# Hybrid decoder step on one core: three of the twelve expert pair loads of the middle rounds are issued by ScalarE instead of SyncE

## What is computed

```
g_logits = (xn @ w_rg) + b_rg;  grp = argmax(g_logits)          # 4 groups
top_v, top_i = top_k(e_logits[grp], 2)                          # 2 of the group's 8 experts
for g in range(4):
    h = silu(einsum('nd,edf->nef', xn, w_gate[g])) * einsum('nd,edf->nef', xn, w_up[g])
    out = out + einsum('nef,efd->nd', h * combine[:, g, :, None], w_down[g])
y = rmsnorm(x + out, g_final)
```

## Time and profile before

| | us |
|---|---|
| median of 3 runs | 1608.3 (1607.51 to 1609.42) |
| time of the profiled execution | 1609.79 |
| span of the profiled execution | 1608.1 |
| TensorE busy | 1423.5 (89%) |
| VectorE busy | 562.4 (35%) |
| ScalarE busy | 407.5 (25%) |

### The profile page before, as it was taken

One profiled execution on the slowest core, in us unless ns is written; L12 is line 12 of the kernel. 1 busy time (PEld: TensorE's weight loads), 2 busy tenths in 40 slices (PEclk: granted clock), 3 DMA queues, 4 the chain that ended last, 5 costly groups with the idle time before them and its releaser, 6 DMA issues.

```text
span 1608.1 us, 24033 instructions
## 1 busy us (share of the span) xinstructions
PE 1423.5 (89%) x9911; PEld 936.3 (58%) x9911; DVE 562.4 (35%) x923; ACT 407.5 (25%) x680; POOL 13.8 (1%) x30
## 2 busy tenths in 40 slices
PE   7999999999999999999977778878878778967967
PEld 7999999999999999963332232322322322412411
DVE  5647765554555555532212112111112111111114
ACT  6454344333333344401201101101102002002003
POOL 0000000000000010000000000000000000000000
PEclk9999999999999999999979989989889888989889
DMA  8777445545555659699999999999999999999997
GB/s 322 301 282 271 148 164 181 180 179 183 182 183 183 255 204 362 235 393 426 431 432 428 433 433 425 436 432 430 432 431 430 430 430 430 431 432 430 434 428 298
DMA packets 42513, 544.73 MB, mean 339 GB/s; under 512 B 5825, under 2 KB 5825, under 8 KB 11593
## 3 DMA queue, kind: packets, MB, share of 16 engines
q1 hardware_dynamic: 42322, 544.03, 82.8%
q10 hardware_dynamic: 144, 0.03, 0.0%
HBM read 540.30 MB, written 3.68 MB: 338 GB/s over the span
## 4 chain that ended last, share of the span: by engine, by line
PE 62%; DMA 34%; DVE 1%; ACT 1%; issue 1%; SPq 0%; DVEq 0%; ACTq 0%
DMA ring<-in_expert_chunks 29%; PE bank L1524 12%; PE bank L1525 12%; PE bank L1526 12%; PE bank L1931 6%; PE bank L1934 5%; DMA side<-in_expert_chunks 4%; PE bank L1811 3%; PE bank L1866 2%; DMA ring<-in_dense_units 1%; PE bank L1858 1%; PE bank L1803 1%; PE bank L1854 1%; PE bank L1847 1%; PE bank L1555 0%
## 5 line engine op out<-in xcount | busy, mean ns | idle before, releaser
L996 DVE TENSOR_TENSOR w_lo<-ring,w_hi 128x1024 fp32r<-128x1024 f32 x220 | 259.8, 1222 | 223.3 <-ACT w_hi L726 222.8
L1524 PE MATMUL bank<-xn_hi,w_hi 128*128 128x264 f32 x1120 | 319.0, 285 | 0.0
L1525 PE MATMUL bank<-xn_lo,w_hi 128*128 128x264 f32 x1120 | 317.3, 283 | 0.0
L1526 PE MATMUL bank<-xn_hi,w_lo 128*128 128x264 f32 x1120 | 317.1, 283 | 0.0
L726 ACT ACTIVATE w_hi<-ring 128x1024 fp32r<-128x1024 f32 x220 | 221.1, 1052 | 367.2 <-PE bank L1526 342.6
L1931 PE MATMUL bank<-side 128*32 128x512 f32 x1024 | 153.5, 741 | 84.4 <-DMA side<-in_expert_chunks 83.4
L1524 PEld LDWEIGHTS bank<-xn_hi,w_hi 128*128 128x128 f32 x1120 | 210.9, 188 | 1.2 <-issue 1.0
L1525 PEld LDWEIGHTS bank<-xn_lo,w_hi 128*128 128x128 f32 x1120 | 211.1, 188 | 0.1
L1526 PEld LDWEIGHTS bank<-xn_hi,w_lo 128*128 128x128 f32 x1120 | 210.0, 187 | 0.0
L1811 PEld LDWEIGHTS bank<-trunk,x_all 128*128 128x128 f32 (+1 forms) x672 | 98.8, 202 | 77.7 <-issue 59.4
L1931 PEld LDWEIGHTS bank<-side 128*32 128x32 f32 x1024 | 33.9, 129 | 178.9 <-DMA side<-in_expert_chunks 98.3
(11 more groups left out here) (309 smaller groups left out, 1640.7 us busy)
## 6 DMA issues: line engine op xcount, KB each, us to landing
ring<-in_expert_chunks SPq DMA_DIRECT2D x33, 4096.0 KB, 33.9
side<-in_expert_chunks SPq DMA_DIRECT2D x28, 4096.0 KB, 38.7
ring<-in_dense_units SPq DMA_DIRECT2D x109, 1024.0 KB, 4.8
trunk<-in_expert_chunks SPq DMA_DIRECT2D x13, 4096.0 KB, 42.9
ring<-in_expert_chunks SPq DMA_DIRECT2D x20, 2048.0 KB, 14.5
ring<-in_expert_chunks SPq DMA_DIRECT2D x18, 1024.0 KB, 18.3
side<-in_expert_chunks SPq DMA_DIRECT2D x8, 2048.0 KB, 10.7
trunk<-in_expert_chunks SPq DMA_DIRECT2D x7, 2048.0 KB, 17.0
```

What stands on the lines that cost most here:

```text
L996: V.tensor_tensor(w_lo[n % 2][:, js, :], raw[n % 2][:, js, :], w_hi[n % 2][:, js, :], ALU.subtract).then_inc(lo_done, 1)
L1524: mm(ps[:, 0:n], w_hi[b][:, j, :], x_hi[:, j, :], start=j == k0, stop=False)
L1525: mm(ps[:, 0:n], w_hi[b][:, j, :], x_lo[:, j, :], start=False, stop=False)
L1526: ins = mm(ps[:, 0:n], w_lo[b][:, j, :], x_hi[:, j, :], start=False, stop=j == k1 - 1)
```

## The change

Of the seven loads in the first loop of SyncE's middle rounds q8 is left out, and of the five in the second q2 and q3; they are issued by ScalarE on its own hardware DMA queue. q4, which stood behind q2 and q3 in SyncE's order and needed no wait there, now waits for chunk 19. ScalarE issues q8 of the round when chunk 7 is used, ahead of the Silu; q2 of the next round after its copy n = 2 (so after chunk 21), q3 after its copy n = 3 (after chunk 23). ScalarE's loop is split into a first round, a loop over the middle ones, and a last round; the first and the last issue no load. The bytes, the places and TensorE's program stay as they are.

```diff
+BY_ACT = (8, 2, 3)
...
                     for q in range(5, PAIRS):
-                        pair_after(q, FREED_BY[q], at, bass.ds(r, 1))
+                        if q not in BY_ACT:
+                            pair_after(q, FREED_BY[q], at, bass.ds(r, 1))
                     for q in range(5):
-                        pair_after(q, AHEAD[q], at, bass.ds(r + 1, 1))
+                        if q not in BY_ACT:
+                            pair_after(q, 19 if q == 4 else None, at, bass.ds(r + 1, 1))
...
+            def pair_by_act(q, round_of):
+
+                s = PAIR_SLOT[q]
+                act.sem_inc(second_in[q], 16)
+                act.dma_start(pair[s].rearrange("p (o n) -> p o n", o=1), pair_v[:, q, round_of, :]).then_inc(full[s], 16)
+
+            def act_round(it, this=None, next=None):
+
+                act.wait_ge(e_used, it * CPR + (CREDIT + 8))
+                if this is not None:
+                    pair_by_act(8, this)
+                nc.scalar.activation(hs, bank[0][:, :], ACT.Silu, scale=slot_rms).then_inc(silu_done, 1)
+                for n in range(4):
+                    act.wait_ge(e_used, it * CPR + (CREDIT + 18 + 2 * n))
+                    if n:
+                        act.wait_ge(sq_done, it * 9 + (3 * n + 1))
+                    nc.scalar.activation(y[:, n % 2, :], bank[2 + n][:, :], ACT.Copy).then_inc(y_ready, 1)
+                    if n >= 2 and next is not None:
+                        pair_by_act(n, next)
...
             with act.Fori(0, npass) as k:
...
+                act_round(k * ROUNDS)
+                with act.Fori(1, ROUNDS - 1) as r:
+                    act_round(k * ROUNDS + r, bass.ds(r, 1), bass.ds(r + 1, 1))
+                act_round(k * ROUNDS + (ROUNDS - 1))
```

More of the change, by code:

```diff
@@ L931, in _ @@
             npass = act.value_load(npass_i[0:1, 0:1], min_val=1, max_val=9)
-            with act.Fori(0, npass) as k:
[L933 to L952, removed]
@@ new lines, in pair_by_act @@
+            def pair_by_act(q, round_of):
[14 more added lines that the diff above has]
+                        pair_by_act(n, next)
+                    if n == 0:
+                        nc.scalar.activation(ssf[:, 2:3], eps_col, ACT.Sqrt)
+                    for t, (p0, p1, _, _) in enumerate(ACC):
+                        if n == 3:
+                            break
+                        q = 3 * n + t
+                        act.wait_ge(aux_done, it * JPR + (A_E + JOB_S[n] + t + 1))
+                        act.wait_ge(sq_done, it * 9 + (q + 1))
+                        nc.scalar.activation(y[p0:p1, 1 - n % 2, :], acc(t, n * 512, (n + 1) * 512), ACT.Square,
+                                             scale=D ** -0.5, accum_out=ssh4[p0:p1, t, n:n + 1]).then_inc(sq_done, 1)
```

## The result

Before 1607.9 us (median of 4 runs), after 1619.77 us (1619.01 to 1620.91, 4 runs): a ratio of 1.0068, 95% interval 1.0056 to 1.0080, so 11.9 us slower. The forecast was 1609.8 with a range up to 1617. The profiled spans are 1608.1 and 1619.2, 11.1 us apart.

The account below looks back on a forecast made before the run. The stream of bytes through the DMA engines was taken to bound the kernel. Bytes, issue times and rate counted 0, holes before q11 +1.5 us: 1608.3 + 1.5 = 1609.8 us, range 1605 to 1617.

Parts of the forecast that it names:

- The three ways: Whole kernel: engines run empty for a while, their rate changes, or the bytes ahead of the last q7 change.
- Order of arrival: Middle rounds: q8 shares the engines from its issue and lands ahead of q7; round length still 12 x 9.71 us.
- halves: Loads on both queues: each queue gets half the engines' rate; q8 takes about 20 us to land instead of 38.
- Rival (d): ScalarE's loads served in order of issue, behind all SyncE has queued; reserve stays, 1608.3 us; chance 0.12.
- The backlog: At q10's and q11's issue: only q9 is ahead of q10; small holes, +1.5 us, bounds 0 and 19.
- Margin 0.6 us: At q10's issue: 12.7 us to landing against 12.1 needed by a load alone, so engines just kept busy.
- rival (a): Queue empty behind q9, TensorE oftener on its lower clock in chunks 14-17: 4 to 19 us, +7 taken; chance 0.20.
- T + 89.5: q8's forecast issue, 89.5 us after the landing T of q7, while SyncE has q6 and q7 queued.
- The 1.5 us of the sum: Behind q10: q11 issued too late in some rounds, 4.3 us over six rounds, of which about a third taken.
- Two rings and the rate: Shared stretches, 58 of 116.5 us a round: no rate change taken, bounds +4.9 and -4.0 us.
- (b): Stretches with two queues: two rings cost rate, up to +4.9 us, 1613; chance 0.06.
- (c): Stretches with two queues: two rings gain rate, each filling the other's pauses, -4.0 us, 1604; chance 0.10.

Follow-up runs that it names:

- the ladders: Kernel before with pairs of 4 MB loads added after its end, the second issued at varied leads; gap between landings 9.7 us, growing below about 4 us lead.
- The three variants: Against the kernel before: only q2 and q3 on ScalarE's queue, +1.3 us; changed kernel with q8 issued later, +1.7; changed kernel with q10 in two 2 MB loads, +3.2.
- the halves: Changed kernel with q10 issued as two 2 MB loads, the first when chunk 14 is used: 1611.9 us against 1608.7 for the kernel before.

## Why the prediction was wrong

**What bounds the kernel: right.** The stream of bytes sets the time, and the end follows q7 of the last round by 53.5 us in both kernels. The three ways in which the time could move were the right ones; the first happened.

**Order of arrival and halves: right.** q8 lands ahead of q7, 23.2 to 23.9 us after its issue, where halves gave about 20 and order of issue would have left 38. The median of all of ScalarE's loads is 24.1 us. TensorE idles 11.52 us before q1 (forecast: some 10). The Trainium skill's rule of turns between rings ("DMA: Bandwidth & Descriptors", Queues, rings and completion order) agrees with this. Rival (d) is out by the same number.

**The backlog: the step that failed.** The prediction found the weak place, q10 behind q9, and priced it: "Margin 0.6 us: the engines are just kept busy." Both terms of that margin were off.

- *The lead.* "A load alone needs its own 9.71 us and a start-and-finish time", 2.4 us. A load alone does take 12.2. But behind a running load it needs about 4 us of lead to follow without a gap, not 2.4. With q10's old issue in round 3, 6.65 us after q7, the lead is 9.71 - 6.65 = 3.1, already short. The 2.0 us that the prediction quotes from the Trainium skill ("DMA: Bandwidth & Descriptors", Anatomy of one DMA) stand in a section on loads that GpSimd issues. SyncE's lone loads of 4 MB show 12.2 - 9.71 = 2.5 here.
- *The issue.* The prediction held q10's issue at 6.65 us and wrote against rival (a) that "the idle before q7 stays about 4 us". It is 7.2 to 11.9 us in the middle rounds. q7 now is the last of q6, q7 and q8, and in round 3 lands 17 us after q6 (1083.03 to 1100.03) instead of 9.7. The forecast had q8 go out at T + 89.5, early enough to take much of its half from q6; in fact it went out 91.2 to 94.7 us after q7's landing and took more of it from q7. When q7 lands, TensorE is at 0.5 of its full clock (windows in the last section), so q10 goes out 6.5 to 7.9 us after q7.

With 4 and a mean of 7.3 the same formula gives 9.71 - 4 - 7.3 = -1.6 us, six times that 9.5. The gaps ahead of q10 show 9.8, most of the 11.1. That the two agree so closely is in part luck: the ladders do not grow one for one below 4 us, and single rounds scatter from 0.6 to 2.2.

**q11: a smaller part, sized too low.** The 1.5 us of the sum were put on q11; it cost 2.7 in the six rounds. Its leads were 3.5 to 5.2 us, all beyond the 2.4 that the sum asked for, so by the sum's own price it would have cost nothing; with a lead of 4.5 us it cost 0.3 in round 3, and with 3.5 us 1.2 in round 4. Chunk 16 ran at 1.92 us in all middle rounds, as forecast. The prediction tied the rounds in which q11 was short to those with a slow chunk 16; before, chunk 16 was slow in round 4 too (3.36 us), where its sum had time to spare.

**Two rings and the rate, rivals (b) and (c): out.** q8 first on one queue costs as much, q2 and q3 on two queues 1.3 us, all three with q8 issued later 1.7 us. The Trainium skill's sentence that several issuing engines save issue time only (same page, Issuing engines are not separate DMA queues) holds here for the rate, to within these 1.3 and 1.7 us, though not for the order.

**Rival (a)** was the true case. It had a chance of 0.20 and a price of 4 to 19 us, put at 7; it is 11 to 12. Its own threshold, a mean of 0.5 us a round, was passed fourfold. Of its chunks 14 to 17, though, it is chunk 14 that ran slowly; 15, 16 and 17 ran at 1.92 to 2.08 us.

**Open.** The three variants in which the loss is largely gone still stand 1.3 to 3.2 us above before. With q8 issued later, q11 goes out only 0.6 us before q10's landing in round 1, and its last piece lands 12.0 us after q10. These 2.2 us too many are about the whole 2.3 by which that profiled span exceeds before. The 118.3 us in round 1 of the halves are not explained: no hole stands ahead of q10 or q11 there. For the rest nothing was tried. Why a load needs more lead behind a running one than alone was not settled either.

## What to carry to other kernels

When the DMA engines bound a kernel, reserve is what counts: at each issue, ask which loads are still in flight, and write the time left in them beside the lead that the next one needs. A load that overtakes others takes from that reserve even if no byte is added, and moving it to a second queue is one way to make it overtake. Price a lead from loads issued behind running ones, not from a load alone, and take the clock after the new wait, not after the old one.

## What the runs showed of the hardware that was not expected

A 4 MB load took 12.2 us alone. On one queue it landed 9.7 us after the load ahead of it in all seven cases with a lead of 4.2 us or more. Issued with a lead of 2.3 us, it took 14.3 us, longer than on engines at rest; on the other queue, with a lead of 2.2, it took 13.5.

TensorE was granted 0.5 of its full clock, 1.2 instead of 2.4 GHz, at the end of an 11 us wait, and kept it into the first matmuls. Windows of 5 us of the changed kernel around q7's landing at 1100.03; the last three columns are granted clock, DMA share and GB/s:

```profile
1085.00:1090.00 5.00, 3.59 (x20) 0.94 (x12) 1.38 (x2) 0.00 (x0) 0.00 (x0) 1.00 0.97 419
1090.00:1095.00 5.00, 0.00 (x0) 0.00 (x0) 0.00 (x0) 0.00 (x0) 0.00 (x0) 0.70 0.97 419
1095.00:1100.00 5.00, 0.00 (x0) 0.00 (x0) 0.00 (x0) 0.00 (x0) 0.00 (x0) 0.50 0.98 419
1100.00:1105.00 5.00, 4.97 (x18) 1.10 (x18) 0.00 (x0) 0.00 (x0) 0.00 (x0) 0.50 1.00 433
1105.00:1110.00 5.00, 3.24 (x25) 0.90 (x28) 2.13 (x3) 0.00 (x0) 0.00 (x0) 0.93 0.86 321
1110.00:1115.00 5.00, 5.00 (x34) 2.32 (x38) 0.42 (x1) 0.00 (x0) 0.00 (x0) 1.00 0.95 400
1115.00:1120.00 5.00, 4.28 (x23) 1.19 (x22) 1.09 (x2) 2.54 (x4) 0.00 (x0) 1.00 0.89 370
1120.00:1125.00 5.00, 5.00 (x36) 1.13 (x34) 0.97 (x2) 1.72 (x6) 0.00 (x0) 1.00 0.95 387
1125.00:1130.00 5.00, 4.20 (x22) 1.23 (x22) 2.06 (x3) 2.14 (x6) 0.00 (x0) 1.00 1.07 454
```

The first is the end of q6's use, at the full clock. The clock is down to 0.5 when q7 lands at 1100.03, and chunk 14 runs at it. The dip of the rate, 321 to 400 GB/s in the four windows from 1105 to 1125, begins as q9 comes to its end and q10 is not yet there, and lasts into the time of q10 and q11.
